# Selecting the first expert pair's rows straight into channel-on-partition form, with the turns of x1 placed around the turns of h2

## The reference, cut to what matters

```python
h = rmsnorm(x, lp['norm2_w']) * (1 + sc2) + sh2
x = x + gt2 * hier_moe(h, lp)
...
for grp in range(N_EXPERT_GROUPS):
    sl = slice(grp * EXPERTS_PER_GROUP, (grp + 1) * EXPERTS_PER_GROUP)
    a = jnp.einsum('td,edf->tef', t, lp['w_gate'][sl])
    u = jnp.einsum('td,edf->tef', t, lp['w_up'][sl])
    act = jax.nn.silu(a) * u * comb[:, sl, None]
    out = out + jnp.einsum('tef,efd->td', act, lp['w_down'][sl])
```

## Time and profile before

| | us |
|---|---|
| median of 3 runs | 1166.89 |
| lowest and highest run | 1166.05, 1170.19 |
| the profiled execution's own time | 1165.01 |
| its span in the trace | 1163.2 |
| PE busy, share of the span | 1040.0, 89% |
| DVE busy, share of the span | 518.4, 45% |
| ACT busy, share of the span | 294.7, 25% |

### The profile page before, as it was taken

One profiled execution on the slowest core, in us unless ns is written; L12 is line 12 of the kernel. 1 busy time (PEld: TensorE's weight loads), 2 busy tenths in 40 slices (PEclk: granted clock), 3 DMA queues, 4 the chain that ended last, 5 costly groups with the idle time before them and its releaser, 6 DMA issues.

```text
span 1163.2 us, 21571 instructions
## 1 busy us (share of the span) xinstructions
PE 1040.0 (89%) x9055; PEld 676.5 (58%) x9055; DVE 518.4 (45%) x1015; ACT 294.7 (25%) x663; POOL 226.6 (19%) x180
## 2 busy tenths in 40 slices
PE   3799999998898788888999799998898989998895
PEld 1699999998554577777555444443333333333342
DVE  1775775304873456666310542433232333333344
ACT  2432334425552233344000420111100111111112
POOL 0554555551240232321000200000000000000000
PEclk9899999998997999998999798999999999999998
DMA  9642442335072500103030788999999999999992
GB/s 360 226 146 73 144 146 84 133 115 212 1 288 75 188 4 4 40 5 129 0 145 1 314 310 326 426 426 425 424 424 427 426 425 423 424 426 426 425 423 111
DMA packets 54013, 277.15 MB, mean 238 GB/s; under 512 B 6712, under 2 KB 14264, under 8 KB 35120
## 3 DMA queue, kind: packets, MB, share of 16 engines
q1 hardware_dynamic: 50400, 268.16, 57.3%
q0 software_dynamic: 3536, 7.85, 1.9%
HBM read 276.16 MB, written 4.72 MB: 241 GB/s over the span
## 4 chain that ended last, share of the span: by engine, by line
PE 62%; DMA 23%; DVE 9%; ACT 3%; issue 2%; SPq 1%; DVEq 0%; ACTq 0%
PE ps L744 18%; DMA ring_b<-in_w_up 16%; PE ps L1192 13%; PE ps L1022 7%; DMA ring_a<-in_w_gate 6%; PE ps L1210 2%; PE ps L683 2%; PE ps L807 1%; DVE temp L1822 1%; PE ps L839 1%; PE ps L945 1%; PE ps L998 1%; PE ps L971 1%; DVE bc L1808 1%; PE ps L848 1%
## 5 line engine op out<-in xcount | busy, mean ns | idle before, releaser
L744 PE MATMUL ps<-h_hi,w_split 128*128 128x392 f32 x768 | 200.0, 341 | 0.0
L1192 PE MATMUL ps<-ring_b,temp 128*64 128x512 f32 x512 | 124.8, 644 | 30.5 <-DMA ring_b<-in_w_up 30.4
L744 PEld LDWEIGHTS ps<-h_hi,w_split 128*128 128x128 f32 x768 | 140.2, 188 | 2.5 <-issue 2.5
L592 POOL TENSOR_TENSOR w_split<-ring_a,w_split 128x1024 fp32r<-128x1024 f32 x46 | 114.8, 2497 | 88.4 <-ACT w_split L1327 88.4
L744 PE MATMUL ps<-h_lo,w_split 128*128 128x392 f32 x384 | 130.8, 341 | 0.0
L1192 PE MATMUL ps<-ring_a,temp 128*64 128x512 f32 x512 | 115.6, 604 | 7.0 <-DMA ring_a<-in_w_gate 6.1
L1210 PE MATMUL ps<-mix,temp 128*64 128x512 f32 x256 | 112.9, 594 | 2.4 <-issue 0.7
L2049 DVE SCALAR_TENSOR_TENSOR temp<-temp,silu_c,ps 128x512 f32<-128x512 f32 x16 | 12.0, 748 | 229.7 <-PE ps L1192 229.7
L1210 PE MATMUL ps<-kv,temp 128*64 128x512 f32 x256 | 113.3, 595 | 0.0
L1192 PEld LDWEIGHTS ps<-ring_b,temp 128*64 128x64 f32 x512 | 38.3, 147 | 115.4 <-issue 74.3
L1192 PEld LDWEIGHTS ps<-ring_a,temp 128*64 128x64 f32 x512 | 42.9, 139 | 76.7 <-issue 76.5
(11 more groups left out here) (331 smaller groups left out, 1668.7 us busy)
## 6 DMA issues: line engine op xcount, KB each, us to landing
ring_b<-in_w_up SPq DMA_DIRECT2D x30, 2048.0 KB, 18.1
ring_a<-in_w_gate SPq DMA_DIRECT2D x28, 2048.0 KB, 17.6
mix<-in_w_down SPq DMA_DIRECT2D x32, 1024.0 KB, 16.5
kv<-in_w_down SPq DMA_DIRECT2D x32, 1024.0 KB, 18.6
ring_a<-in_w_in SPq DMA_DIRECT2D x11, 2048.0 KB, 7.7
ring_a<-in_w_ada SPq DMA_DIRECT2D x6, 2048.0 KB, 9.6
ring_b<-in_w_ada SPq DMA_DIRECT2D x5, 2048.0 KB, 17.8
ring_a<-in_w_gate SPq DMA_DIRECT2D x16, 512.0 KB, 6.0
```

Source lines behind the costliest of these rows:

```text
L592: nc.gpsimd.tensor_tensor(w_split[:, n % 4, 1, :, :], slots[slot_of[load]][:, :, c:c + P], w_split[:, n % 4, 0, :, :].bitcast(fp32), ALU.s ...
L744: last = nc.tensor.matmul(ps[:, 2 + n % 3, 0:ROW], w[:, k, :], h[:, k, :], start=(k == 0 and x == 0), stop=(k == KD - 1 and x == 2))
L1192: last = nc.tensor.matmul(ps[64 * e:64 * e + 64, 2 + n, :], xg_t[:, k, 64 * e:64 * e + 64], slots[2 * n + e][:, k, :], start=(k == 0), sto ...
```

## The change

`select_rows` swaps the operands: a block of 128 channels of `h2_tok` (every eighth element, 128 columns) is the stationary operand and `sel_a` (128 slots) streams through. That gives the turned form at once, in banks 0 and 1, with 8 blocks x 3 token tiles = 24 products in place of 6. The copies to `xg`, the semaphore `rows_selected` and `turn_rows(0)` are gone. `turn_x1(0)` moves ahead of `turn_h2(0)`; `turn_x1(1)` goes ahead of the selection and `turn_x1(2)` behind it; the banks of tiles 1 and 2 are exchanged. The wait for `sel_ready` now stands ahead of `turn_x1(1)`.

```diff
+        X1_BANKS = ((2, 3), (5, 7), (4, 6))
...
+            def turn_x1(t):
+                banks = X1_BANKS[t]
+                for b in range(KD):
+                    last = nc.tensor.transpose(ps[:, banks[b // 4], (b % 4) * P:(b % 4 + 1) * P], x1_t[:, b, t * P:(t + 1) * P], mask("ident"))
+                last.then_inc(x1t_mm, 1)
...
             last.then_inc(lg_mm, 1)
+            turn_x1(0)
             turn_h2(0)
...
             def select_rows():
                 pe.wait_ge(h2t_ready, TT)
-                pe.wait_ge(sel_ready, 1)
-                for n in range(2):
+                for b in range(KD):
                     for t in range(TT):
-                        last = nc.tensor.matmul(ps[:, n, :], sel_a[:, 0, t, :].bitcast(fp32), h2_tok[:, t, n * 512:(n + 1) * 512], start=(t == 0), stop=(t == TT - 1))
-                last.then_inc(h2t_mm, 1)
+                        last = nc.tensor.matmul(ps[:, b // 4, (b % 4) * P:(b % 4 + 1) * P], h2_tok[:, t, :].rearrange("p (i k) -> p k i", k=KD)[:, b, :],
+                                                sel_a[:, 0, t, :].bitcast(fp32), start=(t == 0), stop=(t == TT - 1))
+                last.then_inc(xgt_mm, 1)
...
-            turn_x1(0)
+            pe.wait_ge(sel_ready, 1)
+            turn_x1(1)
             select_rows()
-            turn_x1(1)
-            turn_rows(0)
             turn_x1(2)
...
             turned_x1(0)
-            act.wait_ge(h2t_mm, TT + 1)
-            nc.scalar.copy(xg[:, 512:1024], ps[:, 1, :]).then_inc(rows_selected, 1)
             turned_x1(1)
...
-            dve.wait_ge(h2t_mm, TT + 1)
-            V.tensor_copy(xg[:, 0:512], ps[:, 0, :]).then_inc(rows_selected, 1)
             turned_half(0)
```

More of the change, by code:

```diff
@@ L390, in hybrid_step @@
         rest_dve = sem("rest_dve")
-        rows_selected = sem("rows_selected")
         lg_scaled = sem("lg_scaled")
@@ L1175, in turn_rows @@
             def turn_rows(i):
[L1176 to L1179, removed]
+                pe.wait_ge(xg_in, i * 16)
                 for b in range(KD):
@@ L1541, in turned_x1 @@
                 act.wait_ge(x1t_mm, t + 1)
-                for n, bank in enumerate(((2, 3), (4, 6), (5, 7))[t]):
+                for n, bank in enumerate(X1_BANKS[t]):
                     last = nc.scalar.copy(x1_tok[:, t, n * 512:(n + 1) * 512], ps[:, bank, :])
```

## The result

| | before | changed |
|---|---|---|
| median, us | 1166.62 (6 runs) | 1175.18 (6 runs) |
| lowest and highest | 1164.74, 1170.19 | 1171.12, 1177.02 |
| ratio | 1 | 1.0058 (1.0033 to 1.0083) |
| profiled execution, its time and span | 1165.01, 1163.2 | 1171.12, 1169.2 |

Forecast were 1165.2 us and a range of 1161.8 to 1168.8; the kernel became 0.58% slower by the ratio.

The account below looks back on a forecast made before the run. The expert stage was taken as bound by loads whose first waits for the first expert products. `turn_rows(0)` -1.07, x1 tile 1 -0.87, selection +0.26 made 1.7 us earlier: 1166.89 - 1.7 = 1165.2 us, range 1161.8 to 1168.8.

Parts of the forecast that it names:

- the first term: New selection's 48 records: 47 steps taken as 5.4 us, so it ends 0.26 us later than the old one.
- The unknown is the stationary load itself: Selection's operand stepping by eight elements, without a like row; plain pace taken, bounds from 0.26 us better to 0.224 a record.
- rival 2: Strided stationary loads in the selection's 48 records: 0.7 us slower at 0.165 a record, 3.4 slower at 0.224; chance 0.13.
- The turns' cover: `turn_x1(0)` near 651 us, hidden in PE's waits for ACT before the h2 blocks: costs nothing, 1.3 us if uncovered.
- DVE's copy as what is late next: Copy to `xg_t` directly behind the selection ends last, x1 tile 2 hidden by 0.1 us; first expert products at 672.26.
- One-to-one: Each microsecond by which the first expert products start earlier sends the stage's first load a microsecond earlier.
- Rival 1: Granted clock, low from 702.5 to 712.7 us: 0.85 us faster (chance 0.13) or up to 5.1 faster (0.12).
- Rival 3: Short products with their loads keep the clock low; selection at half pace throughout, 3.7 us slower; chance 0.03.
- Rival 4: Expert-stage loads are bound elsewhere and an earlier first quarter just waits: gain 0.0; chance 0.07.

Follow-up runs that it names:

- the permuted kernel: Changed kernel, complete, with ACT writing each h2 tile in the order the selection reads, so its stationary operand is plain; median 1168.26 us, ratio 1.0010.
- the plain load: Changed kernel with the selection's stationary operand taken as 128 neighbouring elements, channels then in wrong blocks; median 1167.94 us, ratio 1.0002.
- the turns: Kernel before with only the x1 turns moved, with their banks and the `sel_ready` wait; old selection kept; median 1168.34 us, ratio 1.0013.
- the banks: Kernel before with only the accumulator banks of x1 tiles 1 and 2 exchanged; median 1167.70 us, ratio 1.0004.
- the two permuted: Changed kernel with ACT permuting the h2 tiles, ratio 1.0010; and the same with DVE taking half of the last tile, ratio 1.0000.
- the selection alone: Changed kernel with x1 turns put back: tile 0 ahead of the new selection, tiles 1 and 2 behind; median 1175.59 us, ratio 1.0075.
- the selection twice: Changed kernel with its new selection done twice into the same banks; median 1184.61 us, ratio 1.0156.
- the old selection twice: Kernel before with its own selection done twice; median 1175.54 us, ratio 1.0060.

## Why the prediction was wrong

**The step that failed** is the size of the first term, "New: 47 steps between 0.112 and 0.118 are 5.26 to 5.55; I take 5.4". They took 11.3. The step behind it was the choice under **The unknown is the stationary load itself**: "I take the plain pace, for the nearest row is line 1181, whose strided load is as long as line 807's." The loads of the new operand are longer, 334 against 190 ns, and one record follows the next at 0.238 us and not at 0.115. Line 1181 is a transpose, and the product of the selection is not. The prediction compared it to line 807, a true product whose stationary operand is one element repeated 128 times and so has no step at all; the row of a plainly stored one is line 754, at 0.112 us a record. It read the equal 190 ns as "the step is free". Line 1181's own twin is line 1156, a plain transpose with loads of 140 ns, so the step did make the load's record longer; but its turns kept their pace (1.06 against 1.04 us for eight, by the permuted kernel), so that twin too would not have given the price: by its pace nothing, by its loads the 53 ns of rival 2's low end. The rows of the kernel before held none for a true product. The case for rival 2 was there, with the rule of the Trainium skill, page "SBUF — State Buffer", section "Door 1: The DMA port swizzle (why [64,N] ≈ [32,N])", beside it, and got 0.13.

**Rival 2** was the mechanism that came true. Its high end, a load twice as long (0.224 a record, 3.4 us slower), is within 0.9 us of the stretch (4.3 longer). Its low end, 53 ns on top, was no bound from rows of the same kind. The range (to 1168.8) held only the low end. The run with a plain operand leaves no other cause for the 6.05 us in the selection.

**The rest of the sum held.** The turns' cover, DVE's copy as what is late next, and the 1.7 us of the plain load (6.43 against 8.17 in the trace) came out. One-to-one came out within wide intervals, with the doubled selections (11.4 us of stretch, 10.0 measured; 5.2 and 7.0); it may be somewhat more than one, see below.

**The other rivals.** Rival 1, the clock behind pair 0, has a real price, but no trace ties it to the change. The time from the first expert products to the end goes with the mean granted clock of the 75 us behind their start: 487.4 and 488.4 us at 0.98, 488.1 to 489.3 at 0.95, 489.3 to 491.2 at 0.93, and 492.1 to 492.6 at 0.91, over 15 traces. The three traces of the changed kernel have 0.98, 0.91 and 0.91, those with the old chain (the kernel twice, the turns, the banks) 0.93, 0.93, 0.93 and 0.95. So the 1.9 us that the first trace gave back were luck. Rival 3 is excluded by the granted clock of 1.00 in the selection. Rival 4 is excluded by the doubled selections, which cost time.

**The chance** of 0.03 for slower by over 0.5% rested on "none of the cases reaches it". 5.8 us was only 2.4 us away from rival 2's high end. The 4.3 us of the stretch do not reach 5.8 either; it is the excess of the next paragraph that carries the ratio past 0.5%.

**What stays open.** The stretch is 4.3 us longer (0.37%), the three ratios are 1.0058, 1.0070 and 1.0060, about 7.3 us. Two of the three intervals leave 1.0037 out. Kernels with a longer or shorter path measured 1.3 to 3.9 us more than their chains say, those with an unchanged one (the kernel itself, the banks, the turns) 0.5 to 1.5. The old selection doubled (1.9) and the plain load (about 2) have such an excess without a strided load, though each lies within its interval.

The traces do not show where it is. The span less the stretch is 1155.0, 1163.2, 1160.9 and 1157.7 us in the four traces with the old chain and 1156.7, 1161.2 and 1158.8 in the three of the changed kernel, so the means are 1159.2 and 1158.9; with 8 us between traces of one program, 3 us can't be excluded by that.

Part of the scatter is the clock. Over the 16 to 32 runs of the kernel before that belong to each comparison, the time falls by 0.6 to 1.1 us for each 0.001 of the mean granted clock (correlation -0.64 to -0.85). An estimate by the straight line through these runs, at equal clock, puts the kernels with the old chain 0.1 to 0.9 us over before and the three with a shorter one (the plain load, the two permuted) 0.2 to 0.6 over their chains, but the changed kernel still at 5.4 and 6.6 us (chain 4.3), the selection alone at 7.5 (5.2), the selection twice at 19.1 (15.7) and the old selection twice at 7.6 (5.2), each within 1.4 to 2.4 us. By this estimate a delay costs somewhat more than itself (theory E), whatever it is made of; no run was made to test it, and by what wait is not known.

## What to carry to other kernels

When a layout change turns a streamed operand into a stationary one, look at its step in memory: the work may be equal in columns and twice as long in loads. A price must be read from a row of the same kind of instruction. Here neither a transpose with the same step nor a product without one had it. The length of a single load is not the pace of a row of them: transposes with loads of 193 and of 141 ns kept the same pace. Where several traces of one program begin a stage 8 us apart, compare the stage's own length from start to end, and not the spans.

## What the runs showed of the hardware

In these kernels a true fp32 product with a stationary operand of 128 columns loads in 192 ns at a step of 4 bytes, 196 at 8, 330 at 16 and 334 at 32; in a row of products with 128 columns streamed, one record follows the next at 0.112, 0.120, 0.235 and 0.238 us. A transpose with a step of 32 bytes keeps its pace (loads of 193 against 141 ns, 1.06 against 1.04 us for eight). ACT's copy of 128x512 fp32 from the accumulator took 0.59 us with a plain target and 1.08 with a target that scatters in steps of 512 bytes (two in a row 1.9), and DVE's 1.02 where its plain one took 0.69. In two executions of one program the selection began 665.77 and 673.78 us after the start; over 15 traces of these kernels, which do nearly the same work up to there, it began between 665.8 and 674.1.
